# Two steps of the triangular inverse change places, on TensorE and on ScalarE, in a hybrid attention and gated-delta layer

## The reference, cut to what matters

```python
kk = jnp.einsum('bhid,bhjd->bhij', k, k)
a_mat = jnp.where(strict, beta[..., :, None] * decay * kk, 0.0) + jnp.eye(L, dtype=jnp.float32)
eg = jnp.exp(gc)
rhs = beta[..., None] * (v - eg[..., None] * jnp.einsum('bhid,bhde->bhie', k, S))
u = lax.linalg.triangular_solve(a_mat, rhs, left_side=True, lower=True, unit_diagonal=True)
qk = jnp.einsum('bhid,bhjd->bhij', q, k) * decay
o = eg[..., None] * jnp.einsum('bhid,bhde->bhie', q, S) + jnp.einsum('bhij,bhje->bhie', qk, u)
S_new = jnp.exp(gc[..., -1])[..., None, None] * S + jnp.einsum('bhjd,bhj,bhje->bhde', k, w_last, u)
```

## Time and profile before

| | us |
|---|---|
| median of 3 runs | 3533.93 |
| lowest and highest | 3530.08, 3535.12 |
| the profiled execution, device time | 3534.3 |
| its span, first to last instruction | 3532.5 |
| PE busy in it | 3421.8 (97%) |
| PE weight loads | 2904.9 (82%) |
| DVE busy | 1730.3 (49%) |
| ACT busy | 1256.8 (36%) |
| POOL busy | 252.9 (7%) |
| mean granted TensorE clock, share of 2.4 GHz | 0.981 |

### The profile page before, as it was taken

The page is one execution under the profiler, slowest core; times in us unless marked ns, Lnnn a source line. Parts: engine busy times, 40 slices in busy tenths (PEclk is TensorE's granted clock), DMA queues, the critical chain, the costliest instruction groups (busy, mean ns, idle before and its releaser), DMA issues.

```text
span 3532.5 us, 52950 instructions
## 1 busy us (share of the span) xinstructions
PE 3421.8 (97%) x21860; PEld 2904.9 (82%) x21860; DVE 1730.3 (49%) x3115; ACT 1256.8 (36%) x2414; POOL 252.9 (7%) x289
## 2 busy tenths in 40 slices
PE   6979999999999999999999999999999999999998
PEld 6867789999998777888878877888888877788886
DVE  3834335443436654554345744554345755454343
ACT  3322334321224544432234544432223544432222
POOL 1211000000003110000001201000000311000000
PEclk9988899999999999999999999999999999999999
DMA  4101012322233211333333211233334211233332
GB/s 171 60 32 50 25 31 78 104 86 89 84 132 105 68 38 47 114 96 96 96 135 118 69 42 47 87 113 96 96 97 155 79 44 43 76 114 97 96 96 81
DMA packets 88558, 298.66 MB, mean 85 GB/s; under 512 B 12272, under 2 KB 14272, under 8 KB 87664
## 3 DMA queue, kind: packets, MB, share of 16 engines
q1 hardware_dynamic: 88320, 295.28, 26.1%
HBM read 283.63 MB, written 12.62 MB: 84 GB/s over the span
## 4 chain that ended last, share of the span: by engine, by line
PE 52%; issue 11%; ACT 2%; DMA 1%; DVE 1%; SPq 0%; POOLq 0%; POOL 0%; DVEq 0%
PE bank L739 42%; PE bank L927 1%; PE bank L1164 1%; DMA raw<-in_wstream 1%; PE bank L1155 1%; PE bank L1167 1%; PE bank L902 1%; PE bank L1098 1%; PE bank L914 1%; PE bank L1072 1%; PE bank L1078 0%; PE bank L955 0%; ACT junk L1515 0%; PE bank L1000 0%; PE bank L1109 0%
## 5 line engine op out<-in xcount | busy, mean ns | idle before, releaser
L739 PE MATMUL bank<-hnT,wh 128*128 128x512 f32 (+1 forms) x3520 | 931.4, 352 | 0.0
L1680 DVE TENSOR_TENSOR wl<-raw,wh 128x1024 fp32r<-128x1024 f32 x480 | 594.8, 1239 | 657.2 <-ACT wh L1321 655.8
L739 PE MATMUL bank<-xnT,wh 128*128 128x512 f32 (+2 forms) x2560 | 742.0, 376 | 10.0 <-DVE d_dT L1933 5.1
L739 PEld LDWEIGHTS bank<-hnT,wh 128*128 128x128 f32 x3520 | 619.4, 188 | 91.4 <-issue 0.2
L1321 ACT CAST wh<-raw 128x1024 fp32r<-128x1024 f32 x480 | 500.4, 1043 | 391.3 <-PE bank L739 331.3
L739 PE MATMUL bank<-hnT,wl 128*128 128x512 f32 (+1 forms) x1760 | 622.2, 354 | 0.0
L739 PEld LDWEIGHTS bank<-xnT,wh 128*128 128x128 f32 x2560 | 449.5, 194 | 83.1 <-issue 12.9
L739 PE MATMUL bank<-hid,wh 128*128 128x512 f32 (+1 forms) x1760 | 468.3, 354 | 4.3 <-DVE wl L1680 3.2
L739 PE MATMUL bank<-xnT,wl 128*128 128x512 f32 (+2 forms) x1280 | 469.6, 367 | 0.0
L739 PEld LDWEIGHTS bank<-hnT,wl 128*128 128x128 f32 x1760 | 330.6, 188 | 45.8
L739 PEld LDWEIGHTS bank<-hid,wh 128*128 128x128 f32 x1760 | 309.5, 188 | 52.4 <-DVE wl L1680 5.2
(11 more groups left out here) (309 smaller groups left out, 3899.5 us busy)
## 6 DMA issues: line engine op xcount, KB each, us to landing
raw<-in_wstream SPq DMA_DIRECT2D x472, 512.0 KB, 3.5
xr<-in_x_prompt SPq DMA_DIRECT2D x16, 512.0 KB, 5.7
xT<-in_xT SPq DMA_DIRECT2D x4, 2048.0 KB, 12.3
hT<-in_xT SPq DMA_DIRECT2D x4, 2048.0 KB, 8.5
out_yp_out<-hT SPq DMA_DIRECT2D x16, 512.0 KB, 2.9
raw<-in_wstream SPq DMA_DIRECT2D x8, 528.0 KB, 3.6
Sb<-in_state_delta SPq DMA_DIRECT2D x1, 2048.0 KB, 10.6
out_ds_out<-Sb SPq DMA_DIRECT2D x1, 2048.0 KB, 6.8
```

The costliest lines, as they stand in the source:

```text
L739: ins = nc.tensor.matmul(*a, **k)
L1680: v_.tensor_tensor(wl[n % HL][:, 0:m], raw[:, n % RAW, 0:m], wh[n % HL][:, 0:m].bitcast(F32), ALU.subtract).then_inc(sem("lo_done"), 1)
```

## The change

At a level of a 128-row tile PE turns Y first, and then waits for the mask and makes the product. ACT copies X first and the product after it. The same instructions are issued, on the same banks and buffers, and no semaphore is added or dropped. In the tile `"S"` PE's order stays, and only ACT's two copies change places.

```diff
                 for q, l in enumerate(LV[t]):
-                    pe.wait_ge(*made("m_done", lb + q + 1))
                     if q == 0:
                         pe.wait_ge(*made("Y_done", i + 1))
                     else:
                         pe.wait_ge(*made("XY_done", lb + q))
+                    if t != "S":
+                        claim(6, "X_rd", x_turns(t, q))
+                        for h in range(NH // 2):
+                            last = nc.tensor.transpose(bank[6][:, P * h:P * (h + 1)], Y[:, 2 * h:2 * h + 2, :].rearrange("p a n -> p (a n)"), c("ident"))
+                        last.then_inc(sem("X_ps"), 1)
+                    pe.wait_ge(*made("m_done", lb + q + 1))
                     M = q4[f"m{q % 2}"]
...
                     last.then_inc(sem("PT_ps"), 1)
-                    if t != "S":
-                        claim(6, "X_rd", x_turns(t, q))
-                        for h in range(NH // 2):
-                            last = nc.tensor.transpose(bank[6][:, P * h:P * (h + 1)], Y[:, 2 * h:2 * h + 2, :].rearrange("p a n -> p (a n)"), c("ident"))
-                        last.then_inc(sem("X_ps"), 1)
-                    elif q:
+                    if t == "S" and q:
...
                 for q, l in enumerate(LV[t]):
+                    if q or t != "S":
+                        act.wait_ge(*made("X_ps", x_turns(t, q)))
+                        if q:
+                            act.wait_ge(*made("DT_ps", lb + q))
+                        act.copy(X[0:n, :, 0:w], bank[6][0:n, 0:NH * w].rearrange("p (h n) -> p h n", h=NH)).then_inc(sem("X_rd"), 1)
                     act.wait_ge(*made("PT_ps", lb + q + 1))
...
-                    if q or t != "S":
-                        act.wait_ge(*made("X_ps", x_turns(t, q)))
-                        if q:
-                            act.wait_ge(*made("DT_ps", lb + q))
-                        act.copy(X[0:n, :, 0:w], bank[6][0:n, 0:NH * w].rearrange("p (h n) -> p h n", h=NH)).then_inc(sem("X_rd"), 1)
```

## The result

The changed kernel took 3541.0 us, the median of 21 executions (3534.66 to 3543.72); the kernel before, beside it, 3535.36 (3527.82 to 3538.65, 21). The ratio is 1.0016 with the interval [1.001, 1.0022]. That is 5.6 us slower, where the prediction had +2.2. By the bound of 0.2% it still counts as no change, but the interval excludes 1.0006, and the time lies on the upper end of the range. Of the 4.9 us between 3541.0 and the predicted 3536.1, 1.4 come from the kernel before, whose median is 3535.36 here and was 3533.93.

What follows compares the result with a forecast made beforehand. PE's packed stream, busy 97% of the span, was taken as the bound. Terms +1.44, +0.3, +0.76 and -0.28 gave +2.2 us: 3536.5 against the profiled execution, 3536.1 on the median; range 3532 to 3541.

Steps and rivals of the forecast that it cites:

- q = 1: PE from the last matmul ahead to the third behind: 1.46 becomes 1.50 us, +0.04; with q = 2, 32 levels, +1.44.
- q = 3: 16 levels: PE leaves a small shape, enters one and leaves it again, 1.44 becomes 1.63 us, +0.19 each.
- L914 at q = 4: 12 levels with attention: transposes wait for ACT's exponentials, so slack hides most of q = 3's loss; 0.02 each, +0.3 us total.
- no loss at q = 0: 12 levels with attention: L902 waits 0.37 us for the keys' copy, which doesn't move, and PE is ready earlier: 0.
- Rival C: Slower: mask wait and bank claims between short transposes and product cost 0.10 us at 68 levels; 3542.9 us, chance 0.11.
- A: Rival: only the number of shape changes counts, so q = 1 and 2 cost nothing; +1.4 us, 3535.3, chance 0.10.
- B: Rival: order of shapes costs nothing, every weight load equally exposed, only waits change; -0.28 us, 3533.7, chance 0.12.
- D: Rival, faster: PE's X copy waits end altogether and the transposes cost nothing; -4.8 us, 3529.1, chance 0.02.
- Tile 3, q = 4: Four levels with ACT on the path: product copies now end the chain, L1098 starts 0.07 us earlier; -0.28 us total.
- Tile 3, q = 0: ACT is still copying a gate unit when X could be copied, so 0 of the -0.07 us is taken.
- The step that failed: Carrying the sum from the profiled execution (3536.5 us) to the median of runs, 0.4 us lower: 3536.1 us, +0.06%.
- 32, 12 and 4 levels: Level counts in the sum: q = 1 and 2 (+1.44), attention levels (+0.3), tile 3's q = 3 (+0.76) and q = 4 (-0.28).

Runs made afterwards that it cites:

- first group: New order on both engines in the first group only, the other groups as in the kernel before: 3540.45 us, ratio 1.0015.
- two pairs on before: Kernel before, with Y's two transposes made twice at two levels of the first group: 3535.67 us, ratio 1.0003.
- the repeat with four pairs: Second run of the changed kernel with Y's two transposes made twice at four levels of the first group: 3536.14 us, ratio 1.0006.
- four pairs in the second group: Changed kernel with Y's two transposes made twice at four levels, in the second group instead of the first: 3540.14 us, ratio 1.0015.

## Why the prediction was off

**Right.** The prices of a change of shape, step by step: q = 1 1.50 (forecast 1.50); q = 3 a loss of 0.19 in tile 0 and 0.16 to 0.21 in tile 3 (0.19); L914 at q = 4 0.02 later against L902 (0.02); no loss at q = 0; the wait for X gone and one of the same size for PT in its place. Rival C is false: the product stands 0.20 behind the second transpose with the mask's wait and two claims ahead of it, no more than the earlier trace rows. A and B are false, since q = 1 costs 0.04 and q = 3 0.16 to 0.21. D is false, since a wait of the old size stands for the product copy.

**Two terms that were mis-sized.** Tile 3, q = 4: I took -0.07, and it is 1.56 instead of 1.72, -0.16. I had put 0.15 us between the end of the last copy and L1098; behind the second of two short product copies it is 0.06 (1393.22 + 0.27 to 1393.55). Tile 3, q = 0: I took 0, and it is 1.69 instead of 1.78, -0.09. Each is 0.36 us over four groups, so the sum should have been about +1.5 and not +2.2. The executions of the changed kernel with the higher clock lie 1.2 us above the mean of before.

**The step that failed** is the one that carries the sum from the profile to the median: "That execution lies 0.4 us above the median of the three runs; on the median it is 3536.1 us". It takes for granted that the changed kernel is granted the same clock as before, in every execution. No rival and no end of the range spoke of the clock. In the first 560 us TensorE changes between its levels many times (in before the granted clock is 0.89 up to 300 us, 0.85 up to 400, 0.93 up to 500, 0.97 up to 560, and 1.00 behind that), and there a delay of a few tenths of a microsecond isn't worth a few tenths. The sum's 32, 12 and 4 levels also counted the first group like the others. The runs showed in its place: +1.4 in groups 1 to 3, a few tenths of work in the first group, which no run measures apart, and some 6 us more at a lower granted clock (0.978 or 0.979 for 0.980 to 0.982) in 6 of 10 executions.

**What stays open.** Why just that delay brings PE to the stretch at a bad moment wasn't derived. A stretch at 1.2 GHz over L1109, L1114 and L1155 also stands in four profiles of executions that weren't long (first group, two pairs on before, the repeat with four pairs, four pairs in the second group; 921.7 to 923.2 us by the distance above), so that stretch alone doesn't make the 6 us between the two kinds; the longer first part belongs to it. Two profiles of long executions are too few to say whether it is always these two. Nor do the runs separate the moment from a second reading, that more full-array work ahead in tiles 0 to 2 itself spares stretches at 1.2 GHz: every delay was made of such work. The control in the second group excludes only that it helps wherever it stands.

## What to carry to other kernels

Price a reordering by the neighbours' shapes: entering a small tile shape and leaving it each has a price. Long matmuls with only the small block between them take 0.33 + 0.96 = 1.29 us; two transposes add 0.17 directly behind the block (1.46) and 0.21 ahead of it (1.50), so the short full-array instructions stood better behind it. Reordering one engine's half alone can cost as much as both together (here 4.2 and 5.8 against 5.0 to 5.7), so move producer and consumer in one step. Where a kernel has a part in which TensorE's clock changes often, a profile gives the time of one pattern of it; look at the granted clock of every timed execution before a few microseconds are put down to the edit, and test with a harmless delay ahead of that part.

## What was not expected of the hardware

0.9 us of added transposes in the first group made the changed kernel some 3 us faster in the mean; 1.8 us of them on the kernel before cost nothing that could be measured (-1.2 us in the mean). One and the same block of 16 matmuls took 1.11 or 1.97 us in different executions of one kernel. And a DVE sum of 128x4 took 0.70 us instead of 0.15 where POOL's 128x256 instruction ran.
